# First attention: queries as six full tiles, keys ahead of the rotary swap, gate rows inside the attention loop

## The chip, the cores and the metric

One core of a Trainium2 chip. The metric is the device time of one execution in microseconds; three executions of the kernel before gave 1753.39, 1755.93 and 1757.91 us (median 1755.93). The profile is one further execution, taken by the hardware profiler, of 1756.61 us with a span of 1754.80 us between its first and last instruction.

## What is computed

The reference runs a first block (a hybrid of an RWKV recurrence and a latent attention with 8 heads) and then a two-layer second block. The change touches only the latent attention of the first block and one step beside it:

```python
c_q = rms_norm(u_mla[..., :Q_LORA], q_g)                       # 256 tokens x 384
q = einsum('blr,rf->blf', c_q, w_uq).reshape(B, L, 8, 96)      # 64 plain + 32 rotary rows per head
q = concat([q[..., :64], rope_axial(q[..., 64:], *rot)])
...
kv = einsum('blr,rf->blf', c_kv, w_ukv).reshape(B, L, 8, 64 + 64)
k = concat([k_nope, broadcast(k_r)]); v = v                    # 512 keys: 256 tokens + 256 of context
o = softmax(q k^T * 96**-0.5) v                                # per head, 256 queries x 512 keys
x = x + gate * (concat([rw_l, mla_l]) @ w_out)                 # gate: third part of silu(c) @ ada_w + ada_b
```

All numbers are float32. Queries and keys are held transposed: rows of a head on partitions 0 to 95, tokens along the free axis. The rotation of a head's last 32 rows is `q * cos + swap(q) * sin`, where `swap` is a product of those rows with the 32x32 matrix `perm32`.

## The kernel before

The kernel is one block of hand-ordered programs, one for each engine, tied by semaphores (`wait_ge`, `then_inc`). TensorE's program sets most of the order. The weights come through a ring of four slots in SBUF (`slot_wait`), loaded by SyncE; the slots of the query weights are `UQ` and `UQ + 1` (four heads each, 3 x 384 columns), the slot of the key and value weights is `UKV`. `PS` is PSUM, 8 banks of 512 columns.

After the last tile of the input projection (line 2627, tile 27, copied out by ScalarE at line 2835) the steps stand in this order on TensorE:

1. **Gate rows** (line 2634): 8 products of a 128x128 tile with two columns (`SEL`) turn the gate's rows into columns, in bank 7. VectorE adds the bias (line 3072, `gate_added`).
2. **Queries** (line 2645): one head after the other, 96 rows by 256 tokens, 3 products each, into `PS[0:96, h % 4]`. ScalarE copies each to `QM[0:96, h]` (line 2853, `mq_kept`). Heads 4 to 7 wait for the copies of heads 0 to 3.
3. **Swap** (line 2652): waits for all eight copies and `gate_added`; 4 products of `perm32` with two heads' rotary rows, 32 rows by 512 columns, all to partitions 64 to 95, banks 4 to 7. VectorE then does three operations for each pair of heads (lines 3080, 3081, 3083) and raises `roped`.
4. **Keys** (line 2663): heads in pairs on the two column halves, banks 0 to 3, copied by ScalarE (line 2856, `mk_kept`).
5. **Values** (line 2672): 4 tiles of 128 keys by 512, copied by ScalarE (line 2859, `mv_kept`).
6. After waits for `roped` and `mv_kept` 4: **scan values** (line 1947), transposes for the recurrence, copied by ScalarE (line 2864, `vt_kept`), and **chunk sums** (line 1959), to which ScalarE applies exponentials (lines 1969 to 1971).
7. **Attention**: 16 steps `i` (head, half of the queries). TensorE makes scores (line 2687); VectorE takes the maximum (line 3089) and negates it (3091); ScalarE does the exponential (line 2874); VectorE takes the reciprocal and multiplies (3095, 3097); TensorE transposes the probabilities (line 2695) three steps later in its own order; ScalarE copies them (line 406); products with the values follow for each pair of heads (line 419), and VectorE multiplies by the gate of the branch (line 427).

VectorE also spreads the rotated shared key over the eight heads (line 3075) as soon as the first query is made. After attention comes the recurrence (`tensor_scan`), the output projection, and the two layers of the second block. The loads of later weights into the ring start only when the recurrence has ended (`steps_over`).

Of the kernel before, what the change touches and what calls it, by code (L numbers as in the profile page):

```python
# [14 lines left out]
ALU = mybir.AluOpType  # L15
# [97 lines left out]
def over(ap, n):  # L113

    return ap.unsqueeze(1).broadcast_to((ap.shape[0], n, ap.shape[1]))


def along(ap, n):

    return ap.unsqueeze(2).broadcast_to((ap.shape[0], ap.shape[1], n))  # L120


def build(nc, x_h, const0_h, const1_h, const2_h, param1_h, param2_h, meta_h, w1_h, w2_h, out_h):
    with ExitStack() as ctx:
# [87 lines left out]
        SMS, SCAU = [cut(at, 3, 4, P) for at in (4096, 5632)], [cut(at, 2, TX) for at in (7168, 7680)]  # L212
        SCGE, STS = [cut(at, 2, TX) for at in (14080, 13568)], [cut(at, 4, TX) for at in (20736, 21760, 22784, 15616)]
        KR = USH[:, 0, :]
        LSQ, LSK = cut(28928, 3, TX), cut(29696, 2, T1)

        lent = ring[:, :, :].rearrange("p a b -> p (a b)")
# [124 lines left out]
        def weights(n, *shape):  # L342

            return shaped(ring[:, n % RING, 0:int(np.prod(shape))], *shape)
# [4 lines left out]
        def halves(h):  # L349
            return slice(64 * h, 64 * h + 64)  # L350
# [2105 lines left out]
        def _(pe):  # L2456
# [173 lines left out]
                            last = mm(PS[o, i % 4, :], w, HT[:, k, :], start=k < 4, stop=k >= 4)  # L2630
                    last.then_inc(tile_made, 1)
            pe.wait_ge(tile_kept, plain_made(27))
            for i in range(KD):
                last = mm(PS[:, 7, 2 * i:2 * i + 2], ROWSG[:, i // 2, P * (i % 2):P * (i % 2) + P], SEL, start=True, stop=True)
            last.then_inc(gate_rows, 1)
            pe.wait_ge(lat_normed, 1)

            slot_wait(pe, UQ)
            slot_wait(pe, UQ + 1)
            for h in range(8):  # L2640
                if h >= 4:
                    pe.wait_ge(mq_kept, h - 3)
                for k in range(3):
                    w = weights(UQ + h // 4, 3, 384)
                    last = mm(PS[0:96, h % 4, 0:TX], w[:, k, 96 * (h % 4):96 * (h % 4) + 96], REST[:, 4 + k, :],
                              start=k == 0, stop=k == 2)
                last.then_inc(mq_made, 1)

            pe.wait_ge(mq_kept, 8)
            pe.wait_ge(gate_added, 1)  # L2650
            for i in range(4):
                last = mm(PS[64:96, 4 + i, :], perm32[64:96, :],
                          QM[64:96, 2 * i:2 * i + 2, :].rearrange("p h t -> p (h t)"), start=True, stop=True)
            last.then_inc(swap_made, 1)

            slot_wait(pe, UKV)
            w = weights(UKV, 2, 1024)
            for h in range(0, 8, 2):
                if h >= 4:
                    pe.wait_ge(mk_kept, h - 2)  # L2660
                for k in range(2):
                    for j in range(2):
                        last = mm(PS[halves(j), (h + j) % 4, :], w[:, k, 128 * (h + j):128 * (h + j) + 64], KVL[:, k, :],
                                  start=k == 0, stop=k == 1)
                        if k == 1:
                            last.then_inc(mk_made, 1)

            wv = w.rearrange("p k (h t n) -> p k h t n", h=8, t=2)
            for t in range(4):
# [10 lines left out]
            for i in range(19):  # L2680
                if i < 16:
                    h, t = divmod(i, 2)
                    if i >= 4:
                        pe.wait_ge(ms_exp, i - 3)
                    elif i >= 2:
                        pe.wait_ge(vt_kept, i - 1)
                    mm(PS[:, 2 + i % 4, :], QM[0:96, h, P * t:P * t + P], KM[0:96, h, :],
                       start=True, stop=True).then_inc(ms_made, 1)
                if i >= 3:
                    j = i - 3  # L2690
                    h, t = divmod(j, 2)
                    pe.wait_ge(mp_ready, j + 1)
                    pe.wait_ge(mpt_kept, j - 1) if j >= 2 else pe.wait_ge(vt_kept, j + 3)
                    for s in range(4):
                        last = nc.tensor.transpose(PS[:, 6 + j % 2, P * s:P * s + P],
                                                   PM[:, j % 4, P * s:P * s + P], ident)
                    last.then_inc(mpt_made, 1)

                    if t == 0 and h % 2 == 0 and h:
                        mla_products(pe, h - 2)  # L2700
# [52 lines left out]
        def _(act):  # L2753
# [77 lines left out]
            for i, (rows, width, dst, func) in WIN_TILES.items():  # L2831
# [14 lines left out]
                if i == 25:  # L2846
# [103 lines left out]
        def _(dve):  # L2950
# [121 lines left out]
            tt(MOD[:, 16:24, :], PS[:, 7, 0:16].rearrange("p (m c) -> p m c", c=2), along(ada_b[:, 16:24], 2), ALU.add  # L3072
               ).then_inc(gate_added, 1)
            dve.wait_ge(mq_made, 1)
            v.tensor_copy(KM[r, :, :], over(KVL[r, 2, :], 8))

            dve.wait_ge(swap_made, 2)
            for i in range(4):
                q, part = QM[r, 2 * i:2 * i + 2, :], MT1[r, i % 2, :].rearrange("p (h t) -> p h t", h=2)
                tt(part, PS[r, 4 + i, :].rearrange("p (h t) -> p h t", h=2), over(msin[r], 2), ALU.mult)  # L3080
                tt(q, q, over(mcos[r], 2), ALU.mult)
                dr()
                last = tt(q, q, part, ALU.add)
            last.then_inc(roped, 1)

            for i in range(17):
                if i < 16:
                    dve.wait_ge(ms_made, i + 1)
                    v.reduce_max(MNEG[:, i:i + 1], PS[:, 2 + i % 4, :], AX_X)
                    dr()  # L3090
                    ts(MNEG[:, i:i + 1], MNEG[:, i:i + 1], -MLA_SCALE, None, ALU.mult).then_inc(ms_max, 1)
                if i >= 1:
                    j = i - 1
                    dve.wait_ge(ms_exp, j + 1)
                    v.reciprocal(MRS[:, j:j + 1], MSUM[:, j:j + 1])
                    dr()
                    ts(PM[:, j % 4, :], PM[:, j % 4, :], MRS[:, j:j + 1], None, ALU.mult).then_inc(mp_ready, 1)
                    h, t = divmod(j, 2)
                    if t == 1 and h >= 2:
                        mla_out(dve, h - 2)  # L3100
                if i in (8, 10):
                    dve.wait_ge(bon_in, 1)
                    prepare(dve, 0, (i - 8) // 2)
# [171 lines left out]
```

## Time and profile before

| | |
|---|---|
| three runs, median | 1755.93 us (1753.39 to 1757.91) |
| the profiled execution | 1756.61 us, its span 1754.80 us |
| TensorE busy (matmul) | 1690.7 us, 96% of the span |
| TensorE weight loads | 1485.8 us, 85% |
| VectorE, ScalarE, GpSimd busy | 1152.3, 549.0 and 656.9 us |
| chain that ended last, share on TensorE | 86% |
| mean granted TensorE clock | 0.980 |
| the stage touched | 214.66 to 245.94 us, and the attention loop up to 292 us |

In a timeline row the columns are: start in us from the span's start, the time of the group in us, engine, line, operation with output and input, shapes (partitions x elements), number of instructions, and in brackets the idle time before it with what ended it. PE is TensorE's matmul, PEld its weight load, DVE VectorE, ACT ScalarE, POOL GpSimd. A float32 product of the program shows as two MATMUL records.

### The profile page before, as it was taken

The numbers are of one execution on the slowest core, as the hardware profiler recorded it, in microseconds if no ns is written. First come the engines' busy times: TensorE is split into PE (matmuls) and PEld (weight loads), VectorE is DVE, ScalarE is ACT, GpSimd is POOL, SyncE is SP. The second block draws the span as 40 slices with busy tenths as digits, with TensorE's granted clock in tenths as the row PEclk, the third lists the DMA queues.
The fourth block names the chain that finished last, engine by engine and source line by source line (L and its number), as shares of the span: only waits on it lengthen the run. The fifth ranks groups of instructions, "written<-read, shape, count | busy, mean of one in ns | idle before, by whom it ended". The sixth has DMA issues, their size and how long they took to land.

```text
span 1754.8 us, 35997 instructions
## 1 busy us (share of the span) xinstructions
PE 1690.7 (96%) x14736; PEld 1485.8 (85%) x14736; DVE 1152.3 (66%) x2043; ACT 549.0 (31%) x1236; POOL 656.9 (37%) x581
## 2 busy tenths in 40 slices
PE   6999998999899999999999999999999998999999
PEld 3678645998789888878889999989888887999999
DVE  2656235666367789877757664368889796667643
ACT  2223354443353454432321000233554304130100
POOL 1444202564026222113745554254122046545652
PEclk8899998999899999999999999999999999999999
DMA  8332200000353444333344444444343342444443
GB/s 320 135 137 103 96 1 2 4 4 4 125 175 136 138 151 145 121 120 121 123 165 147 167 169 151 162 145 145 120 168 120 133 155 97 168 165 170 168 160 109
DMA packets 53379, 225.71 MB, mean 129 GB/s; under 512 B 5088, under 2 KB 29024, under 8 KB 29280
## 3 DMA queue, kind: packets, MB, share of 16 engines
q1 hardware_dynamic: 53216, 223.40, 36.5%
q8 instruction: 118, 1.93, 0.4%
q14 instruction: 45, 0.37, 0.1%
HBM read 222.34 MB, written 1.05 MB: 127 GB/s over the span
## 4 chain that ended last, share of the span: by engine, by line
PE 86%; DVE 7%; ACT 2%; DVEq 1%; issue 1%; DMA 1%; POOLq 0%; SPq 0%; POOL 0%; ACTq 0%
PE PS L772 18%; PE PS L729 15%; PE PS L1037 15%; PE PS L1061 8%; PE PS L2515 4%; PE PS L2627 3%; PE PS L2049 2%; DVE arena L1444 2%; PE PS L2062 2%; PE PS L2720 1%; PE PS L711 1%; DMA ring<-stream_dram 1%; PE PS L889 1%; PE PS L852 1%; PE PS L1001 1%
## 5 line engine op out<-in xcount | busy, mean ns | idle before, releaser
L772 PE MATMUL PS<-arena,ring 128*128 128x272 f32 (+1 forms) x1664 | 391.5, 390 | 0.4 <-DVE arena L1672 0.4
L772 PEld LDWEIGHTS PS<-arena,ring 128*128 128x128 f32 x1664 | 312.7, 191 | 60.2 <-issue 6.1
L1444 DVE SCALAR_TENSOR_TENSOR arena<-arena,par 128x272 f32<-128x272 f32 (+1 forms) x480 | 260.1, 600 | 7.4 <-issue 0.9
L1884 POOL TENSOR_TENSOR arena<-ring 128x512 f32<-128x512 f32 x48 | 69.4, 1447 | 451.3 <-DMA ring<-stream_dram 388.2
L729 PE MATMUL PS<-arena,ring 128*128 128x136 f32 (+1 forms) x1536 | 201.7, 279 | 1.3 <-ACT arena L1147 1.3
L729 PEld LDWEIGHTS PS<-arena,ring 128*128 128x128 f32 x1536 | 192.3, 191 | 8.0 <-ACT arena L1147 1.7
L729 PE MATMUL PS<-arena 128*128 128x136 f32 (+1 forms) x1152 | 148.0, 280 | 4.4 <-ACT arena L1127 1.5
L1037 PE MATMUL PS<-arena 128*128 128x136 f32 (+1 forms) x1280 | 152.1, 277 | 0.0
L1037 PEld LDWEIGHTS PS<-arena 128*128 128x128 f32 x1280 | 148.7, 191 | 0.0
L729 PEld LDWEIGHTS PS<-arena 128*128 128x128 f32 x1152 | 140.1, 191 | 5.7 <-POOL arena L1884 1.7
L1037 PE MATMUL PS<-arena,ring 128*128 128x136 f32 (+1 forms) x960 | 116.1, 277 | 0.0
L1037 PEld LDWEIGHTS PS<-arena,ring 128*128 128x128 f32 x960 | 112.6, 191 | 0.1
L1166 ACT ACTIVATE arena<-PS 128x272 f32<-128x272 f32 (+1 forms) x80 | 30.8, 389 | 173.7 <-PE PS L772 141.3
L1061 PE MATMUL PS<-arena 128*128 128x136 f32 (+1 forms) x704 | 84.0, 277 | 0.0
L1061 PEld LDWEIGHTS PS<-arena 128*128 128x128 f32 x704 | 81.9, 191 | 0.0
L2304 POOL TENSOR_TENSOR ring<-arena,H 128x256 f32<-128x256 f32 x64 | 45.7, 740 | 87.7 <-ACT arena L2223 87.7
L1411 DVE TENSOR_TENSOR arena<-ring 128x512 f32<-128x512 f32 (+1 forms) x32 | 34.5, 1079 | 64.3 <-DMA ring<-stream_dram 58.8
L1889 POOL TENSOR_TENSOR ring<-ring 128x512 f32<-128x512 f32 x48 | 72.0, 1500 | 0.0
L1886 POOL TENSOR_TENSOR arena<-arena,ring 128x512 f32<-128x512 f32 x48 | 68.6, 1428 | 7.6 <-issue 7.6
L1888 POOL TENSOR_TENSOR arena<-ring,arena 128x512 f32<-128x512 f32 x48 | 66.4, 1384 | 7.6 <-issue 7.6
L1411 POOL TENSOR_TENSOR arena<-ring 128x512 f32<-128x512 f32 (+1 forms) x32 | 40.2, 1256 | 77.5 <-DMA ring<-stream_dram 39.6
L1061 PE MATMUL PS<-arena,ring 128*128 128x136 f32 (+1 forms) x528 | 64.3, 277 | 0.0
(416 smaller groups left out, 2979.9 us busy)
## 6 DMA issues: line engine op xcount, KB each, us to landing
ring<-stream_dram SPq DMA_DIRECT2D x185, 1024.0 KB, 4.8
ring<-stream_dram SPq DMA_DIRECT2D x32, 512.0 KB, 4.4
ring<-stream_dram SPq DMA_DIRECT2D x16, 384.0 KB, 3.6
arena<-x_dram SPq DMA_DIRECT2D x1, 2048.0 KB, 11.7
cst<-const_dram SPq DMA_DIRECT2D x1, 1080.0 KB, 5.0
out_dram<-H SPq DMA_DIRECT2D x4, 256.0 KB, 3.4
cst<-const_dram SPq DMA_DIRECT2D x1, 912.0 KB, 10.3
arena<-stream_dram SPq DMA_DIRECT2D x1, 512.0 KB, 8.5
```

The costliest lines, as they stand in the source:

```text
L729: last = mm(out, w[:, k], tokens[:, k], start=start and k == 0, stop=k == 3, skip_group_check=True)
L772: last = mm(PS[:, 2 * (j % 2) + f, nw], w[:, k, P * f:P * f + P], src[:, k, nw], start=k == 0, stop=k == KD - 1)
L1037: last = mm(out, w[:, k], src[:, k] if tokens is None else src[:, k, tokens], start=k == 0, stop=k == 3)
L1061: last = mm(out, w[:, i], src[:, k] if tokens is None else src[:, k, tokens], start=k == 0 and r in (0, 3, 5), stop=k == 10 and r in (2, 4 ...
L1411: e.tensor_tensor(to[:, 0], a21, a22, ALU.add)
L1444: stt(CVG[:, c, NQ], CVA[:, c, j + Q0:j + T2], dw_w[l][:, c, j:j + 1], CVG[:, c, NQ], ALU.mult, ALU.add)
L1884: g.tensor_tensor(to[:, 0], w21, w22, ALU.add).then_inc(L["summed"], 1)
L1886: g.tensor_tensor(to[:, 1], to[:, 0], w11, ALU.subtract).then_inc(L["summed"], 1)
L1888: g.tensor_tensor(to[:, 2], w12, to[:, 1], ALU.subtract).then_inc(L["summed"], 1)
L1889: g.tensor_tensor(w21, w11, w21, ALU.subtract).then_inc(L["summed"], 1)
L2515: last = mm(out, w[:, k], tokens[:, k], start=start and k == 0, stop=k == 3, skip_group_check=True)
L2627: last = mm(PS[:, i % 4, 0:width], w, HT[:, k, lo:T1], start=k == 0, stop=k == KD - 1)
```

## The change

- The eight query heads are no longer made one by one. The 768 query rows are six tiles of 128 rows: for `i` in 0 to 2 and each weight slot `g`, three products with all 128 columns go to `PS[:, i, 256 g : 256 g + 256]`. Each pair of tiles (one bank) is one `mq_made`.
- ScalarE takes the tiles apart with nine copies (2, 3 and 4 for the three banks), each of both slots at once, 512 columns, from 32 to 96 partitions, some from one group of partitions to another. `mq_kept` counts banks.
- Keys come before the swap. Heads 0 and 1 wait for `mq_kept` 2, heads 2 and 3 for `mq_kept` 3.
- The swap's four products go to four column groups, partitions 32 i to 32 i + 31 of bank 4. VectorE multiplies all of it by `msin` at once into `TURNED` (128x512), multiplies the rotary rows of `QM` by `mcos` in one operation of 32x2048, and, when ScalarE has brought the four pieces of `TURNED` to partitions 64 to 95 (four copies of 32x512 into `PM`, between its copies of the keys and of the values), adds them in one operation of 32x2048.
- The gate rows leave their place ahead of the queries. TensorE makes them in the attention loop at step 3, after that step's scores and ahead of the first transposes; VectorE adds the bias at its step 2, ahead of that step's maximum.

```diff
             pe.wait_ge(tile_kept, plain_made(27))
-            for i in range(KD):
-                last = mm(PS[:, 7, 2 * i:2 * i + 2], ROWSG[...], SEL, start=True, stop=True)
-            last.then_inc(gate_rows, 1)
             pe.wait_ge(lat_normed, 1)
             slot_wait(pe, UQ)
             slot_wait(pe, UQ + 1)
-            for h in range(8):
-                if h >= 4:
-                    pe.wait_ge(mq_kept, h - 3)
-                for k in range(3):
-                    w = weights(UQ + h // 4, 3, 384)
-                    last = mm(PS[0:96, h % 4, 0:TX], w[:, k, 96 * (h % 4):96 * (h % 4) + 96], REST[:, 4 + k, :],
-                              start=k == 0, stop=k == 2)
+            for i in range(3):
+                for g in range(2):
+                    w = weights(UQ + g, 3, 384)
+                    for k in range(3):
+                        last = mm(PS[:, i, TX * g:TX * g + TX], w[:, k, P * i:P * i + P], REST[:, 4 + k, :],
+                                  start=k == 0, stop=k == 2)
                 last.then_inc(mq_made, 1)
-            pe.wait_ge(mq_kept, 8)
-            pe.wait_ge(gate_added, 1)
-            for i in range(4):
-                last = mm(PS[64:96, 4 + i, :], perm32[64:96, :], QM[64:96, 2 * i:2 * i + 2, :] ...)
-            last.then_inc(swap_made, 1)
             slot_wait(pe, UKV)
             for h in range(0, 8, 2):
                 if h >= 4:
                     pe.wait_ge(mk_kept, h - 2)
+                else:
+                    pe.wait_ge(mq_kept, 2 + h // 2)
                 ...
+            for i in range(4):
+                last = mm(PS[32 * i:32 * i + 32, 4, :], perm32[64:96, :], QM[64:96, 2 * i:2 * i + 2, :] ...)
+            last.then_inc(swap_made, 1)
             ... values, scan values, chunk sums, then in the attention loop after the scores of step i:
+                if i == 3:
+                    pe.wait_ge(vt_kept, 4)
+                    for f in range(KD):
+                        last = mm(PS[:, 7, 2 * f:2 * f + 2], ROWSG[...], SEL, start=True, stop=True)
+                    last.then_inc(gate_rows, 1)
                 if i >= 3:
                     j = i - 3
                     pe.wait_ge(mp_ready, j + 1)
+                    if j == 1:
+                        pe.wait_ge(gate_added, 1)
 # ScalarE
-            for h in range(8):
-                act.wait_ge(mq_made, h + 1)
-                a(QM[0:96, h, :], PS[0:96, h % 4, 0:TX], ACT.Copy).then_inc(mq_kept, 1)
+            def keep_queries(i, to, of, first):
+                return a(QM[to, first::4, :], PS[of, i, :].rearrange("p (g t) -> p g t", g=2), ACT.Copy)
+            act.wait_ge(mq_made, 1)   # then 2 copies, mq_kept; mq_made 2: 3 copies, mq_kept; mq_made 3: 4 copies, mq_kept
             ... the copies of the keys
+            act.wait_ge(lat_normed, 2)
+            for i in range(4):
+                last = a(PM[64:96, i, :], TURNED[quad[i], :], ACT.Copy)
+            last.then_inc(lat_root, 1)
 # VectorE
-            dve.wait_ge(gate_rows, 1)
-            tt(MOD[:, 16:24, :], PS[:, 7, 0:16]..., along(ada_b[:, 16:24], 2), ALU.add).then_inc(gate_added, 1)
             dve.wait_ge(mq_made, 1)
             v.tensor_copy(KM[r, :, :], over(KVL[r, 2, :], 8))
             dve.wait_ge(swap_made, 2)
-            for i in range(4):      # part = swap * sin; q = q * cos; q = q + part, on 32 x 512 each
-                ...
+            tt(TURNED..., PS[:, 4, :]..., over(msin, 2), ALU.mult).then_inc(lat_normed, 1)
+            tt(QM[r, :, :], QM[r, :, :], over(mcos[r], 8), ALU.mult)
+            dr()
+            dve.wait_ge(lat_root, 2)
+            tt(QM[r, :, :], QM[r, :, :], PM[r, :, :]..., ALU.add).then_inc(roped, 1)
             ... in the attention loop at i == 2, ahead of the maximum:
+                        dve.wait_ge(gate_rows, 1)
+                        tt(MOD[:, 16:24, :], PS[:, 7, 0:16]..., along(ada_b[:, 16:24], 2), ALU.add).then_inc(gate_added, 1)
```

## Rows read from the trace of the kernel before

**Rows 1.** The page: busy share of the engines; chain that ended last, by engine.

```profile
PE 1690.7 (96%) x14736; PEld 1485.8 (85%) x14736; DVE 1152.3 (66%) x2043; ACT 549.0 (31%) x1236; POOL 656.9 (37%) x581
PE 86%; DVE 7%; ACT 2%; DVEq 1%; issue 1%; DMA 1%; POOLq 0%; SPq 0%; POOL 0%; ACTq 0%
```

**Rows 2.** The chain that ended last, in order of time (start us, us, what): the stage.

```profile
214.66 1.95 PE PS L2634 x16
216.60 10.45 PE PS L2645 x48
227.08 0.39 ACT arena L2853
227.51 3.62 PE PS L2652 x8
231.13 7.02 PE PS L2663 x32
238.14 7.06 PE PS L2672 x16
245.21 0.73 issue
245.94 1.16 PE PS L1947 x32
```

**Rows 3.** Timeline of TensorE and SyncE's queue, 155 to 217 us.

```profile
155.51 48.37 SPq L2441 DMA_DIRECT2D ring<-stream_dram  x7
193.32 1.92 PE L2630 MATMUL PS<-arena,ring 128*32 128x512 f32 x16
207.01 7.17 PE L2627 MATMUL PS<-arena,ring 128*128 128x256 f32 x32
216.46 10.58 PE L2645 MATMUL PS<-arena,ring 128*96 128x256 f32 x48
```

**Rows 4.** Timeline of ScalarE: a query copy, a value copy, the scan values' copies.

```profile
218.01 0.38 ACT L2853 ACTIVATE arena<-PS 96x256 f32<-96x256 f32 x1 [3.41 <-PE PS L2645]
240.09 0.60 ACT L2859 ACTIVATE arena<-PS 128x512 f32<-128x512 f32 x1 [0.71 <-PE PS L2672]
247.13 4.85 ACT L2864 ACTIVATE ring<-PS 64x512 f32<-64x512 f32 x8 [1.28 <-PE PS L1947]
```

**Rows 5.** Groups of VectorE up to 300 us, by form: operations near the new ones.

```profile
L3044 DVE TENSOR_TENSOR arena<-arena 128x2048 f32<-128x2048 f32 x1 | 3.2, 3209 | 0.1
L3080 DVE TENSOR_TENSOR arena<-PS,cst 32x512 f32<-32x512 f32 x4 | 2.7, 683 | 10.9 <-PE PS L2652 10.9
L3050 DVE TENSOR_TENSOR arena<-arena 128x2048 f32<-128x2048 f32 x1 | 2.3, 2284 | 0.0
L3072 DVE TENSOR_TENSOR smalls<-PS,par 128x16 f32<-128x16 f32 x1 | 0.2, 174 | 4.1 <-PE PS L2634 4.1
```

**Rows 6.** Timeline of the first attention steps, 253 to 259 us.

```profile
254.30 2.49 POOL L2291 TENSOR_TENSOR arena<-arena 128x512 f32<-128x512 f32 x2 [60.91 <-ACT arena L1971]
256.99 0.68 DVE L3089 TENSOR_REDUCE smalls<-PS 128x1 f32<-128x512 f32 x1
257.13 0.66 PE L2695 MATMUL PS<-c,arena 128*128 128x128 f32 x4 [2.52 <-DVE arena L3097]
258.59 0.66 PE L2695 MATMUL PS<-c,arena 128*128 128x128 f32 x4
```

**Rows 7.** Windows (us, PE, PEld, DVE, ACT, POOL busy, granted TensorE clock, DMA share, GB/s).

```profile
254.60:257.13 2.53, 0.01 (x2) 0.01 (x1) 1.31 (x3) 1.78 (x6) 2.19 (x2) 1.00 0.00 0
286.00:290.00 4.00, 3.31 (x18) 1.90 (x18) 0.50 (x2) 1.19 (x2) 0.00 (x0) 0.59 0.02 4
297.00:314.00 17.00, 17.00 (x332) 16.77 (x332) 7.92 (x24) 4.72 (x16) 8.62 (x12) 0.50 0.01 3
```

**Rows 8.** The chain that ended last: 32 records in the recurrence at two times.

```profile
302.62 1.71 PE PS L2062 x32
...
333.42 1.05 PE PS L2049 x32
```

More of the change, by code:

```diff
@@ L214, in build @@
         KR = USH[:, 0, :]
+        TURNED = cut(37120, 512)
         LSQ, LSK = cut(28928, 3, TX), cut(29696, 2, T1)
@@ L2632, in _ @@
             pe.wait_ge(tile_kept, plain_made(27))
-            for i in range(KD):
-                last = mm(PS[:, 7, 2 * i:2 * i + 2], ROWSG[:, i // 2, P * (i % 2):P * (i % 2) + P], SEL, start=True, stop=True)
-            last.then_inc(gate_rows, 1)
             pe.wait_ge(lat_normed, 1)
@@ L2639, in _ @@
             slot_wait(pe, UQ + 1)
-            for h in range(8):
-                if h >= 4:
-                    pe.wait_ge(mq_kept, h - 3)
-                for k in range(3):
-                    w = weights(UQ + h // 4, 3, 384)
-                    last = mm(PS[0:96, h % 4, 0:TX], w[:, k, 96 * (h % 4):96 * (h % 4) + 96], REST[:, 4 + k, :],
-                              start=k == 0, stop=k == 2)
-                last.then_inc(mq_made, 1)
-            pe.wait_ge(mq_kept, 8)
-            pe.wait_ge(gate_added, 1)
-            for i in range(4):
-                last = mm(PS[64:96, 4 + i, :], perm32[64:96, :],
-                          QM[64:96, 2 * i:2 * i + 2, :].rearrange("p h t -> p (h t)"), start=True, stop=True)
-            last.then_inc(swap_made, 1)
+            for i in range(3):
[4 more added lines that the diff above has]
+                                  start=k == 0, stop=k == 2)
+                last.then_inc(mq_made, 1)
             slot_wait(pe, UKV)
@@ L2666, in _ @@
                             last.then_inc(mk_made, 1)
+            for i in range(4):
+                last = mm(PS[32 * i:32 * i + 32, 4, :], perm32[64:96, :],
+                          QM[64:96, 2 * i:2 * i + 2, :].rearrange("p h t -> p (h t)"), start=True, stop=True)
+            last.then_inc(swap_made, 1)
             wv = w.rearrange("p k (h t n) -> p k h t n", h=8, t=2)
@@ L2688, in _ @@
                        start=True, stop=True).then_inc(ms_made, 1)
+                if i == 3:
+                    pe.wait_ge(vt_kept, 4)
+                    for f in range(KD):
+                        last = mm(PS[:, 7, 2 * f:2 * f + 2], ROWSG[:, f // 2, P * (f % 2):P * (f % 2) + P], SEL,
+                                  start=True, stop=True)
+                    last.then_inc(gate_rows, 1)
                 if i >= 3:
@@ L2850, in _ @@
                     a(MT1[:, 0, 0:TX], MT1[:, 0, 0:TX], ACT.Exp, scale=-0.5).then_inc(lat_root, 1)
-            for h in range(8):
-                act.wait_ge(mq_made, h + 1)
-                a(QM[0:96, h, :], PS[0:96, h % 4, 0:TX], ACT.Copy).then_inc(mq_kept, 1)
+            def keep_queries(i, to, of, first):
+                return a(QM[to, first::4, :], PS[of, i, :].rearrange("p (g t) -> p g t", g=2), ACT.Copy)
+            quad = [slice(32 * i, 32 * i + 32) for i in range(4)]
+            act.wait_ge(mq_made, 1)
+            keep_queries(0, slice(0, 96), slice(0, 96), 0)
+            keep_queries(0, quad[0], quad[3], 1).then_inc(mq_kept, 1)
+            act.wait_ge(mq_made, 2)
+            keep_queries(1, quad[1], quad[0], 1)
+            keep_queries(1, quad[2], quad[1], 1)
+            keep_queries(1, halves(0), halves(1), 2).then_inc(mq_kept, 1)
+            act.wait_ge(mq_made, 3)
+            keep_queries(2, quad[2], quad[0], 2)
+            keep_queries(2, quad[0], quad[1], 3)
+            keep_queries(2, quad[1], quad[2], 3)
+            keep_queries(2, quad[2], quad[3], 3).then_inc(mq_kept, 1)
             for h in range(8):
@@ L3070, in _ @@
             dr()
-            dve.wait_ge(gate_rows, 1)
-            tt(MOD[:, 16:24, :], PS[:, 7, 0:16].rearrange("p (m c) -> p m c", c=2), along(ada_b[:, 16:24], 2), ALU.add
-               ).then_inc(gate_added, 1)
             dve.wait_ge(mq_made, 1)
@@ L3077, in _ @@
             dve.wait_ge(swap_made, 2)
-            for i in range(4):
[L3079 to L3084, printed above, removed]
+            tt(TURNED.rearrange("p (h t) -> p h t", h=2), PS[:, 4, :].rearrange("p (h t) -> p h t", h=2), over(msin, 2),
+               ALU.mult).then_inc(lat_normed, 1)
+            tt(QM[r, :, :], QM[r, :, :], over(mcos[r], 8), ALU.mult)
+            dr()
+            dve.wait_ge(lat_root, 2)
+            tt(QM[r, :, :], QM[r, :, :], PM[r, :, :].rearrange("p i (h t) -> p (i h) t", h=2), ALU.add).then_inc(roped, 1)
             for i in range(17):
@@ L3088, in _ @@
                     dve.wait_ge(ms_made, i + 1)
+                    if i == 2:
+                        dve.wait_ge(gate_rows, 1)
+                        tt(MOD[:, 16:24, :], PS[:, 7, 0:16].rearrange("p (m c) -> p m c", c=2), along(ada_b[:, 16:24], 2),
+                           ALU.add).then_inc(gate_added, 1)
                     v.reduce_max(MNEG[:, i:i + 1], PS[:, 2 + i % 4, :], AX_X)
```

## The prediction

> **What bounds the kernel now.** I read the page first: TensorE is busy for 96% of the span, and 86% of the chain that ended last lies on it [rows 1]. So an edit is worth what it takes off TensorE's own path, as long as nothing else becomes late. Then the chain in order of time over the stage of the change [rows 2]. The reader is to see that it is one unbroken run on TensorE from 214.66 to 245.94 us, 31.28 us long: gate rows, queries, a short step through ScalarE's last query copy, swap, keys, values, and 0.73 us for the last value copy ahead of the scan values. VectorE and ScalarE have no other place in it. Last the timelines of the single engines, for what hides beside that path and what a new wait would find there [rows 3 to 6], and the windows with the granted clock [rows 7].
>
> **Gate rows.** Their 16 records go from 214.66 and the queries' chain takes over at 216.60; the queries' own row starts at 216.46 [rows 3], so 1.80 us leave the path. They go to a place after the scores of step 3, where TensorE stands idle for 2.53 us (254.60 to 257.13) until VectorE's first product is there [rows 6, 7]. 1.80 to 1.95 us fit with 0.6 us to spare, so they cost nothing there on TensorE. Were that cover gone they would cost their full 1.9. VectorE's addition, 0.17 us [rows 5], comes into its loop ahead of the third maximum at 256.99. There VectorE and TensorE go with the same step, 1.46 us from one transpose group to the next [rows 6], so the addition has no cover: nothing to 0.17 us, I take 0.15. Queued behind the new wait on VectorE are the maximum of step 2 and with it ScalarE's exponential, but the gate columns are made by about 256.5 on the old clock, 0.5 us before VectorE asks.
>
> **Queries.** Before: 48 records. Line 2627 has the new shape, 128x128 weights with 256 columns: 32 records from 207.01, of which the span without the tail is 6.97 us, 0.218 each [rows 3] (7.17 less some 0.2 of the last one's pipeline). The old shape gives the same, 10.45 / 48 = 0.218 [rows 2]. After: 3 x 2 x 3 products x 2 = 36 records, 7.85 us. They start at 214.66, end at 222.51. This saves 12 x 0.218 = 2.6 us.
>
> **Query copies and the new wait.** ScalarE starts some 0.25 us after a group's end (first query: 6 records from 216.46 [rows 3] end at 217.77, the copy starts at 218.01 [rows 4]). A copy of 512 columns is 0.60 us with 128 partitions and 4.85 / 8 = 0.606 with 64, crossing from one half to the other [rows 4], so I take 0.605 for the new ones. Bank 0 is ready at 217.28, bank 1 at 219.90, bank 2 at 222.51. Copies: 217.5 to 218.7, 220.15 to 221.97, 222.76 to 225.18. Keys 0 and 1 need the second count, at 221.97: no wait, they run from 222.51 to 224.27 (7.02 / 4 = 1.755 a pair [rows 2]). Keys 2 and 3 need the third, and start at 225.23: **a new stall of about 0.95 us** behind which keys, swap and values are all queued. It takes the place of the old wait before the swap (0.5 us, 227.0 to 227.51). Should the strided, cross-group copies take 0.8 us each, it would be 1.75; were they as fast as the 0.38 us of 256 columns [rows 4], 0.05. The other three pairs: 5.27 us, to 230.50. Their copies stay ahead of the waits by about 0.25 us (keys 3 and 4 copied by 228.45, the last pair asks at 228.74).
>
> **Swap.** Before 8 records one after the other, 3.62 us [rows 2], all on one column group. The trace of before has no 32x32 products side by side, but line 2630 has 32-column products on four column groups with four different streams on the same partitions: 16 records in 1.92 us [rows 3], 0.12 each for 0.43 alone. So 8 records cost 0.96 us; that is the nearest row and my value. Upper bound 3.6 (no overlap), lower 0.86 (two full passes of 0.43). Saved: 2.65. It ends at 231.46.
> The Trainium skill, "TensorE: Matmul & The Clock Gate", part 3, says that a weight load passes a running product only when its row group differs, and the four swaps share row group 64 to 95. By that rule eight loads would stand bare and the swap would cost near 1.8; line 2630 shares all its rows and shows no such cost, so the row decides.
>
> **Rotation off the path.** VectorE starts some 0.2 us after the swap: 231.65. `TURNED` 0.68 us, to 232.3 [rows 5]. Its product with `mcos` has 2048 columns: 2.28 us as line 3050, up to 3.21 as line 3044 [rows 5]; partitions don't matter. ScalarE meanwhile has finished the keys' copies (231.9), waits for VectorE at 232.3 (behind this new wait are the value copies), does four copies to 234.8, then the value copies. The first value tile is ready at 233.4, so that one copy is 1.5 us late, the second 0.4, and from the third on ScalarE is on time again. VectorE's addition goes from 234.9 to 237.2, `roped`. TensorE asks for it only with the last value copy.
>
> **Values.** From the value group to the scan values it was 245.94 - 238.14 = 7.80 us [rows 2], with 0.07 for the tail that the chain still counts to the keys: 7.87. Again so: 231.46 + 7.87 = 239.33. `roped` is 2.1 us early; with both long operations at 3.21 us it would be at 239.1, still just in time.
>
> **The sum.** Stage before 31.28, after 24.67 (7.85 + 1.755 + 0.95 + 5.27 + 0.96 + 7.87): **6.6 us less**. Item by item: gate rows -1.8, queries -2.6, swap -2.65, waits +0.45. From 245.94 on all shifts: ScalarE's 4.85 us of copies and what follows start with the first scan values [rows 4], GpSimd has been idle for 60.91 us waiting for ScalarE [rows 6], and SyncE's last load, UKV, was issued by 203.88 [rows 3], 18.6 us before the keys ask for it, while its next waits for the end of the recurrence. Nothing stands still in absolute time, so the gain goes to the end whole, less 0.15 in the loop: **6.5 us**. The profiled execution, 1756.61 with 1.81 of it outside the span, becomes 1750.1. The median of the runs is 0.68 lower; on it the time is **1749.4 us**, 0.37% less.
>
> **Rivals.**
> - *The clock decides.* The granted clock is 1.2 GHz in most of 286 to 290 and 2.4 again, then 1.2 for all of 297 to 314 [rows 7], after TensorE had gaps in its last attention steps. 32 records took 1.71 us in it and 1.05 later [rows 8], so those 17 us cost up to 17 x 0.66 / 1.71 = 6.6. The change shifts the loop against whatever places these stretches. Half of such a stretch more or less moves the time by 3 to 4 us; the three runs spread over 4.5 us already. On the bad side I get 1753.5, within 0.3%; on the good side 1746.
> - *The swap's four products don't overlap*, because their rows are the same 32: 2.65 us lost, `roped` at 239.9 adds 0.6, in all 1752.7. For it: no row shows this very tile. Against it: line 2630.
> - *Copies bind.* ScalarE's nine plus four copies at 0.8 us: stall +0.8, last key pairs +0.6, `roped` still in time: 1750.8. This bends the forecast, and stays faster by 0.3%.
> - *Slower than before: the clock falls at the new stall.* At 224.3 TensorE stops for 0.95 us with the first keys done, where before there was no gap longer than 0.73 between 214.66 and 254.6. If that dropped the clock to 1.2 GHz up to the scan values, the remaining keys, swap and values (12.2 us of products) would take 12.2 more, scan values included 16: 1759 to 1762. It decides if the clock is down for more than 6.5 us of full work. Against it: 2.53 us of idleness at 254.6 left the clock at full, and so did the gaps of 0.5 and 0.73.
>
> **Chances.** Forecast (5.3 to 8 us gained) 0.66; a helpful clock beyond that 0.05; clock against, 1751 to 1754.5, 0.17; swap without overlap 0.05; a gain lost somewhere I don't see, near zero change, 0.04; slower by the stall's clock or a late wait 0.03. Measurement can tell about 0.3%, 5.3 us. So faster by more than that 0.71, within 0.26, slower 0.03. The range reaches from 1746.5 (the good clock) to 1753.5 (the bad one, and the swap in series).
>
> **What would show it.** Line 2645's successor with 36 records in about 7.9 us; a gap of about 1 us after the first 8 key records, ended by ScalarE's query copies; the swap's 8 records in about 1 us; the addition at the end of the rotation before 238 us; first scan values at 239.3; gate rows inside a gap that ends as before with VectorE's product; the first transposes at 250.5. The prediction is wrong if the swap shows 3.5 us, if copies of 32 partitions are much over 0.6 us, if TensorE's wait ahead of the scan values ends with VectorE, or if the stretches of low clock are of another length than 3 plus 17 us.

## The result, and the profile after

The changed kernel takes 1743.86 us in the median of four runs (1741.65 to 1744.63), the kernel before 1756.12 (1753.39 to 1757.91): ratio 0.9929, 95% interval 0.9912 to 0.9947. That is 12.3 us less, where 6.5 were forecast, and below the range of 1746.5 to 1753.5. The profiled execution has a span of 1742.8 us against 1754.8. Further sets of runs, told of below, put the gain at 10.2 us (means of 24 and 117 runs: 1743.9 +- 0.5 and 1754.0 +- 0.3, standard errors). Each set was run on one chip, with runs of the kernel before beside it, and the sets are from several chips. Taken set by set, without the first one, the gain is 9.8, 9.5 and 9.4 us.

The page of the kernel after; it answers to [rows 1], with the mean granted clock of the core under it (0.980 before).

```profile
PE 1681.3 (96%) x14724; PEld 1481.6 (85%) x14724; DVE 1147.8 (66%) x2034; ACT 554.9 (32%) x1241; POOL 658.2 (38%) x581
PE 86%; DVE 7%; ACT 3%; DVEq 1%; issue 1%; DMA 1%; SPq 0%; POOL 0%; ACTq 0%
core 0: 1742.8 us, clock 0.984
```

The chain that ended last, kernel after, the stage (start us, us, what); it answers to [rows 2].

```profile
213.62 8.05 PE PS L2642 x36
221.69 0.58 ACT arena L2858
222.29 0.59 ACT arena L2858
222.89 0.59 ACT arena L2858
223.49 0.60 ACT arena L2858
224.14 5.37 PE PS L2655 x24
229.51 0.99 PE PS L2661 x8
230.50 7.06 PE PS L2669 x16
237.56 0.73 issue
238.29 1.16 PE PS L1948 x32
```

The stage runs from 213.62 to 238.29: 24.67 us, the 24.67 of the prediction's sum, against 31.28 before. Queries (L2642) in 36 records, four query copies (L2858) as the wait ahead of keys 2 and 3, swap (L2661) in 0.99 us instead of 3.62, values as before.

So the surprise is elsewhere. Reading the same instructions in both traces, the kernel after leads by this much:

| at | before, us | after, us | lead, us |
|---|---|---|---|
| first input projection product (L2627, L2628) | 155.3 | 154.3 | 1.0 |
| first scan values (L1947, L1948) | 245.9 | 238.3 | 7.6 |
| last products of attention (L419, L420) | 290.4 | 282.6 | 7.8 |
| recurrence over, next products (L2710, L2715) | 458.2 | 451.0 | 7.2 |
| end of the output projection (L2720, L2725) | 496.4 | 486.3 | 10.1 |
| first layer, line 889, 890 | 670.1 | 660.4 | 9.7 |
| first layer, line 993, 994 | 915.4 | 903.4 | 12.0 |
| last product (L1061, L1062) | 1750.5 | 1738.5 | 12.0 |

The stage gives 6.6. Another 1.0 is there before anything changed (the first stretch of low clock lasts 6.8 us in this trace and 10.2 in the other), 2.9 appear in the output projection and 2.3 between 670 and 915 us, all in code that is the same in both. Windows there, in the columns of [rows 7] (the last three are granted clock, DMA share, GB/s); first two of the kernel before, then the same work in the kernel after:

```profile
464.00:468.00 4.00, 3.60 (x9) 2.95 (x10) 3.79 (x9) 0.00 (x0) 0.00 (x0) 0.57 1.02 430
839.70:843.10 3.40, 3.40 (x14) 3.17 (x15) 2.04 (x4) 2.20 (x3) 0.00 (x0) 0.50 0.41 173
```

```profile
456.00:460.00 4.00, 4.00 (x19) 3.54 (x20) 3.90 (x8) 0.00 (x0) 0.00 (x0) 1.00 1.01 420
828.00:832.00 4.00, 3.45 (x27) 3.37 (x28) 2.99 (x6) 2.20 (x3) 0.92 (x2) 1.00 0.52 221
```

The kernel before stands at 1.2 GHz in both places (0.50 in the second window, and 0.57 in the first, where the low stretch is 3.4 of the 4 us), the kernel after at 2.4 (1.00). At the output projection a load also landed sooner. TensorE's wait for the first output weights, kernel before, then kernel after:

```profile
464.39 4.45 PE L2720 MATMUL PS<-arena,ring 128*128 128x256 f32 x12 [2.42 <-DMA ring<-stream_dram]
```

```profile
455.94 2.86 PE L2725 MATMUL PS<-arena,ring 128*128 128x256 f32 x12 [1.27 <-DMA ring<-stream_dram]
```

Of the 2.9 us gained there 1.15 are the shorter wait and 1.6 the twelve records behind it (4.45 us against 2.86). The two go together in the other traces as well. In the five traces in which this wait is 2.1 us or longer (before, before_again, before_pad_4, pad_4, filled) the clock is then at 1.2 GHz for 3.4 us and the twelve records take 4.2 to 4.5 us; in the fourteen with a wait of 1.5 us or less they take 2.86. The wait is 2.4 and 2.1 us in the two traces of the kernel before, and 1.1 to 1.3 in the four of the changed kernel. Why the load lands later in some executions no run shows.

Adding up all stretches of low clock gives 68.6 us in the trace of before and 54.7 in that of after. Each run lists its span and mean clock, so the time at low clock, 2 x (1 - clock) x span, is known for every run of every kernel here. Over 264 runs of fifteen kernels the time is well described by a constant for the kernel plus **0.37 us for each us at low clock** (what is left scatters by 1.6 us). That is the yardstick for the experiments. The last column gives the constants of the same fit when each set of runs has an offset of its own, with the first set left out; their standard errors are 0.4 to 0.9 us.

| kernel | runs | mean time, us | at low clock, us | the kernel's constant, against the changed kernel | the same, with an offset for each set |
|---|---|---|---|---|---|
| before | 117 | 1754.0 +- 0.3 | 68.1 +- 0.6 | +7.6 | +7.3 |
| after | 24 | 1743.9 +- 0.5 | 61.3 +- 1.4 | 0 | 0 |
| gate_back | 12 | 1746.1 +- 0.7 | 64.0 +- 1.8 | +1.2 | +1.2 |
| queries_by_head | 12 | 1747.8 +- 0.8 | 65.5 +- 2.2 | +2.3 | +2.5 |
| swap_one_group | 6 | 1746.9 +- 0.5 | 62.2 +- 1.9 | +2.6 | +2.9 |
| split_copies | 6 | 1743.3 +- 0.4 | 61.0 +- 1.2 | -0.5 | -0.3 |
| pad_4, pad_8, pad_12 | 6, 12, 12 | 1748.0, 1748.8, 1751.8 | 65.2, 62.3, 65.3 (+- 2 to 3) | +2.6, +4.6, +6.5 | +1.5, +3.4, +5.3 |
| after_padded, padded_again | 23 | 1753.4 +- 0.8 | 65.7 +- 1.8 | +7.9 | +7.5 |
| before_pad_4 | 11 | 1758.9 +- 1.0 | 71.6 +- 2.0 | +11.2 | +9.9 |
| before_filled | 6 | 1744.7 +- 1.5 | 43.6 +- 2.4 | +7.4 | +7.0 |
| filled | 6 | 1738.2 +- 1.1 | 45.2 +- 2.0 | +0.4 | +0.7 |
| filled_split | 5 | 1738.8 +- 0.8 | 45.9 +- 1.3 | +0.7 | +0.3 |
| filled_more | 6 | 1735.0 +- 1.5 | 42.2 +- 3.1 | -1.7 | +0.1 |

### The profile page after: what moved, and what is told of

Same layout as the page of the kernel before. It is cut to its first block, busy times and chain, and to the rows that moved or that the text cites. A ratio compares the mean times of both kernels' runs of the same rounds, so it can differ in the third digit from the quotient of the medians.

```text
span 1742.8 us, 35968 instructions
## 1 busy us (share of the span) xinstructions
PE 1681.3 (96%) x14724; PEld 1481.6 (85%) x14724; DVE 1147.8 (66%) x2034; ACT 554.9 (32%) x1241; POOL 658.2 (38%) x581
## 3 DMA queue, kind: packets, MB, share of 16 engines
HBM read 222.34 MB, written 1.05 MB: 128 GB/s over the span
## 4 chain that ended last, share of the span: by engine, by line
PE 86%; DVE 7%; ACT 3%; DVEq 1%; issue 1%; DMA 1%; SPq 0%; POOL 0%; ACTq 0%
PE PS L773 19%; PE PS L730 15%; PE PS L1038 15%; PE PS L1062 8%; PE PS L2516 5%; PE PS L2628 3%; PE PS L2050 2%; PE PS L2063 2%; DVE arena L1445 2%; PE PS L712 1%; PE PS L2725 1%; DMA ring<-stream_dram 1%; PE PS L890 1%; PE PS L853 1%; PE PS L1002 1%
## 5 line engine op out<-in xcount | busy, mean ns | idle before, releaser
L1062 PE MATMUL PS<-arena 128*128 128x136 f32 (+1 forms) x704 | 84.0, 277 | 0.0
L1062 PEld LDWEIGHTS PS<-arena 128*128 128x128 f32 x704 | 81.9, 191 | 0.0
L2305 POOL TENSOR_TENSOR ring<-arena,H 128x256 f32<-128x256 f32 x64 | 45.9, 746 | 87.7 <-ACT arena L2224 87.7
L1889 POOL TENSOR_TENSOR arena<-ring,arena 128x512 f32<-128x512 f32 x48 | 65.7, 1368 | 7.6 <-issue 7.6
L1062 PE MATMUL PS<-arena,ring 128*128 128x136 f32 (+1 forms) x528 | 64.3, 277 | 0.0
## 6 DMA issues: line engine op xcount, KB each, us to landing
arena<-x_dram SPq DMA_DIRECT2D x1, 2048.0 KB, 12.2
```

The costliest lines, as they stand in the source:

```text
L1062: last = mm(out, w[:, i], src[:, k] if tokens is None else src[:, k, tokens], start=k == 0 and r in (0, 3, 5), stop=k == 10 and r in (2, 4 ...
L1889: g.tensor_tensor(to[:, 2], w12, to[:, 1], ALU.subtract).then_inc(L["summed"], 1)
```

## The experiments

**Is it luck? Both kernels again.** No edit in after_again, after_third, after_fourth and before_again.

> The changed kernel once more, unaltered. Theory A (chance): the stage itself gave the 6.6 us that its rows show, the other 5.5 us came from stretches of low clock that fell elsewhere by luck. Then this repeat gives a ratio of 0.995 to 0.997, and the sum of low-clock stretches in its trace differs from the 54.6 us of the first trace. Theory B (systematic): whatever gives the other 5 us belongs to the change, and the ratio is 0.992 to 0.994 again.

> The kernel before once more, unaltered: ratio 1.000, and how wide the ratio of two identical kernels is. In its trace, theory A expects the starts of the low-clock stretches at another offset from the span's start than in the first trace of it, and another sum than 68.4 us; theory B expects the same stretches (286.8, 297.0, 464, 840 us) again.

after_again: 1743.01 us, ratio 0.9937 (0.9915 to 0.9959). before_again: 1752.78, ratio 0.9991 (0.9974 to 1.0007). The ratio is the one that theory B wanted (0.992 to 0.994), but its interval covers theory A's too. The trace of after_again has 65.3 us at low clock where the first had 54.7 (a new stretch of 13.7 us at 322 us), and is 3.1 us longer: one profiled execution of this kernel is not repeatable in its clock, and the first trace of after was a kind one. That of before_again shows the stretches of the first trace of before within 0.1 us up to 843 us, 70.1 us in sum.

> The changed kernel a third time, to tell whether its time at low clock (60.1 us in the mean of 12 runs so far, against 68.8 in 58 runs of the kernel before) is really less. If it was chance, the mean of the new runs is 66 to 70 us and the time 1746 to 1747. If it is a property of the kernel, 58 to 62 us and 1743 to 1744.

> The changed kernel, unaltered, on another chip's time. If the mean low clock of 60.8 us is its own, again 58 to 63 us and 1743 to 1745 us. If it was a low draw and the true value is that of the padded ones, 63 to 66 us and 1745 to 1746 us.

after_third: 1745.35, ratio 0.9946 (0.9931 to 0.9962); after_fourth: 1742.56, ratio 0.9944 (0.9930 to 0.9958). Low clock is 62.2 us in after_third, just above the 58 to 62 of a property of the kernel and below the 66 to 70 of chance, and 62.7 in after_fourth, inside the 58 to 63 of the first reading; the times fit neither reading's range. Together the 24 runs have 61.3 +- 1.4 us at low clock against 68.1 +- 0.6. The difference, 7 us, is beyond chance; by the yardstick it is worth 2.6 us. Without the first four runs, which raised the question, the 20 others have 62.2 +- 1.5, and set against the kernel before that ran beside them they have 6.3, 7.1 and 3.8 us less, worth 1.4 to 2.6 us. Of the 7.6 us in the constant the stage explains 6.6. For the last us the traces have one row of that size, the wait for the first output weights, 1.1 us longer in the mean of the two traces of the kernel before than in the four of the changed one; two and four traces don't prove it.

**Only the time taken off? The same time put back.**

```diff
+            for i in range(15):
+                mm(PS[:, 3, 0:TX], weights(UQ, 3, 384)[:, 0, 0:P], REST[:, 4, :], start=True, stop=True)
             for i in range(3):
                 for g in range(2):
```

> The changed kernel with 15 useless products (30 records of 128 x 256, 6.5 us by the 0.218 us each) ahead of its queries: all that follows comes as late as in the kernel before. If only the time saved in the stage counts, it is at the kernel before, 1755 to 1757. If part of the gain comes from how the changed stage and attention loop are built, it keeps some 4 to 5 us of gain, 1750 to 1752. If the gain hangs on the place in time at which the recurrence arrives, it loses all 12 us.

> The changed kernel with the 15 useless products ahead of its queries a second time. By time alone it is 6.7 us above the changed kernel, 1750.6. If an arrival 6.7 us later at the recurrence also costs clock, low clock is again 66 to 71 us in the mean and the time 1754.

after_padded: 1755.05, ratio 1.0004 (0.9987 to 1.0020); padded_again: 1753.03, ratio 0.9986 (0.9970 to 1.0002). The 30 records took 6.74 us of the chain and the query records behind them 0.27 less, so the stage with them is 31.14 us, 6.47 longer and near the 31.28 of before. But the mean of the 23 runs is 9.5 us above the changed kernel and near the kernel before. With the same arrival the two kernels cost nearly the same, so no gain sits in the new loop as such. Of the 3.0 us that come on top of the 6.47, 1.6 are 4.4 us more at low clock, and 1.4 stay without a cause, or 1.0 +- 0.5 with an offset for each set. One window of the trace of after_padded shows a single stretch of 27.3 us at 1.2 GHz where most others have 17 (pad_8 has one of 27.3 too, after_third two of 10.2):

```profile
286.97:314.27 27.30, 24.13 (x403) 21.62 (x406) 11.16 (x30) 6.12 (x19) 10.98 (x14) 0.50 0.01 3
```

**Does the low clock depend on the arrival?** The same products, 4, 8 and 12 of them, and 4 in the kernel before. The expectations set two theories against each other: by the arrival theory the time at low clock hangs on the moment at which the later stages are reached, by the loop theory on how the changed stage and attention loop are built.

> The changed kernel with 4 useless products (8 records, 1.75 us) ahead of its queries. Arrival theory: half a 3.4 us step later, so the sum at low clock moves by more than 4 us from the 60.8 of the changed kernel, either way, and the time is off 1744.3 + 1.75 = 1746.1 by 2 us or more. Loop theory: low clock stays at 60 to 62 us, the time is 1746.1.

> The same with 8 products (3.5 us, about one whole step). Arrival theory: the low clock is as in the changed kernel, 61 us, and the time 1744.3 + 3.5 = 1747.8. Loop theory: the same. So this run tells only if the low clock is neither: then arrival in absolute time, later is worse, would be the reading.

> The same with 12 products (5.2 us, one and a half steps). Arrival theory: low clock as with 4 products. Loop theory: 61 us and 1749.5.

> The kernel before with 4 useless products (1.75 us) ahead of its queries. Arrival theory: its low clock leaves 69 us by more than 4 us, in the same direction as with 4 products in the changed kernel. Loop theory: 69 us, and 1754.2 + 1.75 = 1756.0.

pad_4: 1748.07, ratio 0.9956 (0.9941 to 0.9971). pad_8: 1748.51, 0.9964 (0.9951 to 0.9976). pad_12: 1751.35, 0.9983 (0.9969 to 0.9996). before_pad_4: 1758.21, 1.0026 (1.0013 to 1.0039). Low clock 65.2, 62.3, 65.3 and 71.6 us: within their errors of 2 to 3 us this is neither a clean up and down with the shift, as the arrival theory wanted, nor flat at 61. All padded forms lie above the changed kernel. The constants follow the pads: by their traces' stages 1.7, 3.5, 5.2 and 6.5 us were put in, and 2.6, 4.6, 6.5 and 7.9 are found, about 1 more. With an offset for each set they are 1.5, 3.4, 5.3 and 7.5, so most of that 1 us belongs to the set in which pad_4, pad_8 and pad_12 ran (no run of the changed kernel stands beside them). Every kernel with the new order has less low clock in the mean (61 to 66 us, those with filled waits left out) than the two with the old one (68 and 72). Why, stays open.

The trace of before_pad_4 has a stretch of 6.8 us at low clock from 232.72, in the middle of the stage, and swap and keys take 3.3 us more by it (4.13 and 9.85 us in the chain, against 3.62 and 7.02 in [rows 2]). TensorE had not been idle: it was busy for 17.12 of the 17.59 us before, its longest gap was 0.47 us, and it was 3 us into the swap's eight 32x32 records in one column group. The windows ahead of the fall and in the stretch:

```profile
215.13:232.72 17.59, 17.12 (x79) 11.81 (x80) 2.46 (x2) 3.04 (x8) 0.00 (x0) 1.00 0.00 1
232.72:239.55 6.83, 6.83 (x16) 1.71 (x16) 5.42 (x9) 1.19 (x2) 0.00 (x0) 0.50 0.00 0
```

**One part undone at a time.**

```diff
 # gate_back: the gate rows, VectorE's addition and its semaphore at their old places
             pe.wait_ge(tile_kept, plain_made(27))
+            for i in range(KD):
+                last = mm(PS[:, 7, 2 * i:2 * i + 2], ROWSG[...], SEL, start=True, stop=True)
+            last.then_inc(gate_rows, 1)
 # queries_by_head: eight heads of 96 rows with eight copies; keys wait for mq_kept 6 and 8
 # swap_one_group: products to the old place, VectorE's twelve operations of before
-                last = mm(PS[32 * i:32 * i + 32, 4, :], perm32[64:96, :], ...)
+                last = mm(PS[64:96, 4 + i, :], perm32[64:96, :], ...)
```

> The changed kernel with the gate rows back ahead of the queries. By the sum of the prediction it costs 1.8 us and gives back 0.15: 1.65 us slower than the changed kernel, 1745.5. If filling TensorE's wait in the attention loop also keeps the clock up later, it costs more, 3 to 6 us.

> The changed kernel with the queries again as eight heads of 96 rows (48 records, eight copies of 256 columns); keys first, swap on four column groups and gate rows in the loop stay. By the records: 12 x 0.218 = 2.6 us more on TensorE, but the stall before keys 2 and 3 (0.6 us in the trace) is gone: 2.0 us slower in the stage. The stall before the first keys should be about 0.5 instead.

> The changed kernel with the swap's four products again one after the other on one column group, and VectorE's twelve operations instead of the rotation through ScalarE. By the records the swap grows from 0.99 to 3.6 us: 2.6 us slower in the stage; the rotation then ends some 10 us after the swap began and is just ahead of the wait before the scan values. If those waits bind, it is 0.5 to 1 us more.

gate_back: 1745.62, ratio 0.9954 (0.9939 to 0.9969); its stage is 26.45 us, 1.8 more than in the changed kernel, its constant 1.2 more, which is what the sum had put and not the 3 to 6 us of the other reading. queries_by_head: 1747.26, ratio 0.9961 (0.9946 to 0.9976); stage 26.40, 1.7 more, constant 2.3. It has no stall ahead of the keys at all, rather than the 0.5 us I had put there. swap_one_group: 1747.19, ratio 0.9957 (0.9943 to 0.9971); stage 27.46, 2.8 more, constant 2.6. Its chain ends in a place that no other kernel here has:

```profile
230.51 3.56 PE PS L2661 x8
...
239.39 0.68 DVE arena L3099
240.07 0.61 DVEq L3098
240.68 0.60 DVE arena L3097
...
241.35 0.69 DVE arena L3099
242.09 1.17 PE PS L1948 x32
```

With the swap in one column group TensorE waits for VectorE's rotation, not for the value copies, but by 0.2 us only, where the expectation had put 0.5 to 1. The three parts sum to 1.8 + 1.7 + 2.8 = 6.3 us of the 6.6: **each is worth what its records say**.

**The stall ahead of keys 2 and 3.** Two of the last four query copies go to VectorE.

```diff
+            dve.wait_ge(mq_made, 3)
+            for of, to in ((slice(64, 96), slice(32, 64)), (slice(96, 128), slice(64, 96))):
+                last = v.tensor_copy(QM[to, 3::4, :], PS[of, 2, :].rearrange("p (g t) -> p g t", g=2))
+            last.then_inc(lat_normed, 1)
```

> The changed kernel with two of the last four query copies on VectorE, which is idle there. ScalarE is then ready 1.2 us earlier, the stall of 0.6 us before keys 2 and 3 goes: 0.6 us faster in the stage, in the times hardly to be told from the changed kernel.

1743.20 us, ratio 0.9938 (0.9923 to 0.9952). In its chain queries and keys join with nothing between, and the stage is 23.84 us, 0.83 less; the times can't tell it from the changed kernel:

```profile
213.11 8.04 PE PS L2642 x36
221.15 7.02 PE PS L2657 x32
228.16 0.99 PE PS L2663 x8
```

**The quiet ahead of the recurrence.** Useless products where TensorE waits: three ahead of a transpose near the end of attention, one and two about its last products, five ahead of the first level of the recurrence.

```diff
+            for _ in range(5):
+                nc.tensor.matmul(PS[:, 1, 0:256], ones, c0[:, 0:256], start=True, stop=True)
             for n in range(NCH + 1):
```

> The changed kernel with eleven useless products of 128 x 256 (0.44 us each) put into gaps in which TensorE waits, at the end of attention and ahead of the first level of the recurrence. If low clock in the first rounds of the recurrence (17 us in every trace so far) comes from the quiet ahead of it, this stretch goes or shrinks to 3 to 7 us and the time falls by 3 to 6 us. If it comes from the small products of these rounds themselves, the stretch stays and the time is the same or up to 1 us longer.

> The kernel before with the same eleven useless products. If the quiet ahead of the recurrence alone sets the 17 us stretch, whatever stands in the attention stage, it gains as much as the changed kernel did, 5 to 6 us: 1748 to 1749, with the 17 us stretch gone from its trace. If the new stage is what lets the clock stay, it gains nothing.

> The useless products in the gaps and the two query copies on VectorE together. If the two gains are independent: 0.8 us below the kernel with the products alone, 1736.8, some 17 us below the kernel before. In the trace the stage takes 23.8 us and there is no 17 us stretch of low clock after attention.

> The changed kernel with the eleven useless products, two query copies on VectorE, and three more useless products (1.3 us) in TensorE's wait for the first output weights (1.27 to 2.4 us in the traces). If low clock at some 460 us comes from that wait, it no longer appears and the time is 1 us below the kernel without these three, 1737 to 1738; if the wait is shorter than 1.3 us in a run, they cost up to 0.3 us.

filled: 1737.57, ratio 0.9908 (0.9891 to 0.9924). before_filled: 1744.20, ratio 0.9943 (0.9924 to 0.9962). filled_split: 1738.79, ratio 0.9906 (0.9890 to 0.9922). filled_more: 1734.95, ratio 0.9904 (0.9886 to 0.9921). Windows ahead of and in the first rounds, kernel after, then filled:

```profile
283.00:288.00 5.00, 1.91 (x64) 1.77 (x64) 3.72 (x8) 0.77 (x2) 2.88 (x4) 1.00 0.01 3
290.00:300.00 10.00, 10.00 (x172) 9.78 (x172) 4.12 (x13) 2.95 (x11) 4.87 (x6) 0.50 0.01 3
```

```profile
283.00:288.00 5.00, 5.00 (x90) 4.03 (x89) 3.72 (x8) 0.77 (x2) 3.43 (x5) 1.00 0.00 0
290.00:300.00 10.00, 9.75 (x324) 9.25 (x320) 8.04 (x25) 4.60 (x16) 6.98 (x9) 1.00 0.01 3
```

In the trace of the kernel after TensorE works for 1.91 of 5 us and the clock is then down for 17.07 us (288.64 to 305.71); with the gaps filled it stays at 2.4 GHz and does 324 records where it did 172. The kernel before shows the same in [rows 7], and before_filled over its window 297 to 314:

```profile
297.00:314.00 17.00, 16.57 (x526) 15.45 (x523) 11.30 (x34) 9.07 (x30) 13.44 (x17) 1.00 0.01 4
```

That is 526 records against 332. All sixteen traces without the useless products have a stretch of 10 us or more at low clock that begins between 279 and 305 us, the four with them have none. The gain, 5.7 us on the kernel after and 9.4 on the kernel before in the means, does not need the new stage. On the kernel before it is more than the 5 to 6 us expected: the mean time at low clock falls by 24.5 us, and in the trace of before_filled the stretches of 3.4 us at 286.75 and 464.25 are missing beside the one of 17. The constants are those of the unfilled kernels: the products cost next to nothing and, by the yardstick, all of the gain is clock. The copies on VectorE added nothing that the times can tell (filled_split). filled_more has the lowest median of all, and in its trace no stretch of low clock lies between 56 and 816 us; but against the kernel before that ran beside it on the same chip its ratio is that of filled, and its constant with an offset for each set is +0.1. Which of the three filled kernels on the new stage is best the runs can't tell; each is 16 to 17 us below the kernel before that ran beside it.

## Why the prediction was right and wrong

- **The stage: right in every term to 0.16 us.** From start to start (predicted in brackets): queries 7.97 us (7.85), the first key pair with the new stall 2.55 (2.71), the other pairs 5.37 (5.27), swap 0.99 (0.96), values and the wait at their end 7.79 (7.87), in sum 24.67 (24.67). That the sum is met to the last digit is luck: errors of 0.12 and 0.16 us cancel. All four traces of the changed kernel show 24.67 to 24.68. The stall itself is 0.61 us where 0.95 was put, since the queries end 0.1 later and the first pair, once alone on TensorE, shows 1.94 us and not 1.755. The trace of before had the side-by-side products at the wrong shape only, and the nearest row gave the right price.
- **The Trainium skill's rule** on weight loads within one row group ("TensorE: Matmul & The Clock Gate", part 3) did not show: the eight weight loads, all on one row group, went within 0.15 us beside the running products, and the swap took 0.99 us, not 1.8.
- **Rotation: right.** VectorE's long operations took 2.28 us each, and its addition ended at 236.15 by the timeline, 2.1 us ahead of the first scan values at 238.29.
- **Gate rows: right, and the 0.15 us put down for the loop did not show.** They stand in the gap, and VectorE's addition took 0.16 us. From the first scan values to the last products of attention it is 44.3 us, before 44.4, each with one stretch of 3.4 us at low clock; in filled and before_filled, with none, 43.17 and 43.11. Timeline of the kernel after:

```profile
246.80 1.84 PE L2689 MATMUL PS<-cst,H 128*128 128x2 f32 x16
249.37 0.16 DVE L3110 TENSOR_TENSOR smalls<-PS,par 128x16 f32<-128x16 f32 x1
249.50 0.66 PE L2700 MATMUL PS<-c,arena 128*128 128x128 f32 x4 [0.85 <-DVE arena L3120]
```

- **"so the gain goes to the end whole, less 0.15 in the loop": here it failed.** Nothing was lost on the way, but the sum has no term for the clock after the stage; it stands there at nothing. In the mean the changed kernel is 7 us less at low clock, which is worth 2.6 us (1.4 to 2.6 in the later sets by themselves). The prediction had seen these stretches, but took them as a rival with a symmetric risk of 3 to 4 us and a 5% chance of a helpful clock, and read them from a single trace. Even so its good end was too tight: 6.6 from the stage and 4 from a clock better by 10 us give 1745 for a single run, and single runs of the changed kernel lie between 1738.8 and 1748.0.
- **The starting point was a high draw.** The forecast subtracts from 1755.93, the median of three runs; 117 runs of the kernel before have a mean of 1754.0. Of the 5.5 us between forecast (1749.4) and result (1743.9), 1.9 are this, 2.6 the clock, and 1.0 is not explained; the longer wait for the first output weights is a row of that size, but not shown to be the cause. In the same way 2.1 of the first comparison's 12.3 us are luck.
- **The rival of the slow end** (clock down at the new stall) was wrong for the changed kernel, in all four of its traces. Its price was also too low by its own rows: keys, swap and values behind the stall are 5.27 + 0.96 + 7.06 = 13.3 us, not 12.2. A fall of the clock inside the stage does occur, in the old order with 1.75 us of products ahead (before_pad_4), and its mean time rose by 4.8 us. But there it came behind no stall, in the middle of the swap's small products.
- **The price of low clock.** The prediction took 0.66 / 1.71 = 0.39 us for each us from two different lines in [rows 8]. The same line, 2062, took 1.71 us at low clock and 1.05 at 314.98, so the value stands, and the runs gave 0.37.
- **The size of the forecast.** A gain of 6.5 against 10.2 in the long run; the term that was mis-sized is the clock, put at 0 and worth 2.6, beside the 1 us above.

## What to carry to other kernels

The path's own rows priced this reordering to 0.16 us or better in each term, even for a tile shape that the trace has only in a neighbour. But where TensorE's clock drops in stretches, forecast the time at low clock as a term of its own, from the mean clock of many runs and not from one trace, and multiply by a slope (here 0.37). Take the starting point from many runs too. And look for what the stretches follow: eleven useless products in waits bought 5.7 us on the changed kernel, and 9.4 on the kernel before, nearly as much as the whole reordering.

## What the runs showed of the hardware

- Runs of the same kernel differ by up to 14.7 us (the kernel before, 1747.6 to 1762.3), and most of what separates them goes with the time at low clock: 0.37 us for each us, near the 0.39 that the 17 us stretch gives when priced from its records in [rows 8] (0.66 / 1.71).
- Stretches of low clock in the traces were 3.4, 6.8, 10.2, 13.7, 17.1 or 27.3 us long. The one of 17.1 us in the first rounds of the recurrence stood in a dense flow of small products, 332 records in the 17 us of [rows 7], and still did not end sooner.
- Useless 128 x 256 products of two constants, written to a free bank of PSUM, kept the clock at 2.4 GHz through TensorE's waits at the end of attention and in the rounds after them, in four traces of four.
- The clock can fall with no long idle time ahead: in before_pad_4 it fell after TensorE had been busy for 17.12 of the 17.59 us before, 3 us into eight 32x32 products in one column group.
